# Six buffers for the split weights, and splits three quanta ahead of TensorE

## The reference

```python
xn = rmsnorm(x, norm_mix_pre)
p = (xn @ w_in).astype(f32)
p_rwkv, p_qkv, p_z, p_beta, p_alpha, p_gate_a, p_gate_b = _split(p, IN_SPLITS)
...
y = rwkv7_recurrence(rh, rwkv_heads(decay), kh, vh, -kk, kk * ah)
...
o = gated_delta_rule_chunked(q, k, gdn_heads(v), g, beta)
...
mixed = jax.nn.sigmoid(p_gate_a) * y_a + jax.nn.sigmoid(p_gate_b) * y_b
x = x + rmsnorm(mixed.astype(x.dtype) @ w_out, norm_mix_post)
xn = rmsnorm(x, norm_ffn_pre)
hidden = jax.nn.silu(xn @ ffn_w_gate) * (xn @ ffn_w_up)
return x + rmsnorm(hidden @ ffn_w_down, norm_ffn_post)
```

## Time and profile before

| what | us |
|---|---|
| median of 3 runs | 2353.65 |
| lowest and highest run | 2353.6 and 2360.31 |
| the profiled execution, its own time | 2358.39 |
| its span, first to last instruction | 2356.5 |
| PE busy | 2161.3 (92%) |
| DVE busy | 1414.1 (60%) |
| ACT busy | 1086.9 (46%) |

### The profile page before, as it was taken

One profiled execution on the slowest core, in us unless ns is written; L12 is line 12 of the kernel. 1 busy time (PEld: TensorE's weight loads), 2 busy tenths in 40 slices (PEclk: granted clock), 3 DMA queues, 4 the chain that ended last, 5 costly groups with the idle time before them and its releaser, 6 DMA issues. The chain is left out here.

```text
span 2356.5 us, 51465 instructions
## 1 busy us (share of the span) xinstructions
PE 2161.3 (92%) x19523; PEld 1862.1 (79%) x19523; DVE 1414.1 (60%) x2772; ACT 1086.9 (46%) x2019; POOL 158.2 (7%) x277
## 2 busy tenths in 40 slices
PE   5699999999999999999999966939999999999995
PEld 5698888888888888888888854838888888878884
DVE  3276687778677766867776754444554544444444
ACT  4354555545554545555454533344444444434443
POOL 2000110110011011101101110000000000000000
PEclk8699999999999999999999966969999999999998
DMA  4654545444444545444544304426655555545452
GB/s 114 155 143 116 138 111 132 123 125 125 115 116 123 129 113 139 113 113 123 130 114 113 87 5 185 154 90 197 195 182 192 181 192 182 174 165 191 178 184 101
DMA packets 388239, 327.32 MB, mean 139 GB/s; under 512 B 15360, under 2 KB 328160, under 8 KB 381408
## 3 DMA queue, kind: packets, MB, share of 16 engines
q1 hardware_dynamic: 376304, 319.16, 46.5%
q10 hardware_dynamic: 11760, 5.41, 0.9%
HBM read 322.44 MB, written 2.10 MB: 138 GB/s over the span
## 5 line engine op out<-in xcount | busy, mean ns | idle before, releaser
L1489 DVE TENSOR_TENSOR wlo<-wr,whi 128x1024 fp32r<-128x1024 f32 x296 | 362.4, 1225 | 436.0 <-ACT whi L1484 436.0
L232 PE MATMUL ps<-hi,xh 128*128 128x384 f32 (+1 forms) x1600 | 581.7, 364 | 42.8 <-DVE lo L218 24.4
L234 PE MATMUL ps<-hi,xl 128*128 128x384 f32 (+1 forms) x1600 | 548.9, 343 | 0.0
L233 PE MATMUL ps<-lo,xh 128*128 128x384 f32 (+1 forms) x1600 | 548.1, 343 | 0.0
L1484 ACT ACTIVATE whi<-wr 128x1024 fp32r<-128x1024 f32 x296 | 313.5, 1060 | 493.2 <-PE ps L1502 484.9
L218 DVE TENSOR_TENSOR lo<-raw,hi 128x768 fp32r<-128x768 f32 (+1 forms) x400 | 378.1, 964 | 147.6 <-ACT hi L213 144.0
L213 ACT ACTIVATE hi<-raw 128x768 fp32r<-128x768 f32 (+1 forms) x400 | 328.1, 834 | 245.8 <-PE ps L234 235.4
L232 PEld LDWEIGHTS ps<-hi,xh 128*128 128x128 f32 x1600 | 311.1, 194 | 76.4 <-issue 47.7
L1498 PE MATMUL ps<-whi,xh 128*128 128x512 f32 x832 | 328.1, 394 | 20.5 <-DVE wlo L1489 20.5
L1502 PE MATMUL ps<-whi,xl 128*128 128x512 f32 x832 | 326.9, 393 | 0.0
L1500 PE MATMUL ps<-wlo,xh 128*128 128x512 f32 x832 | 326.5, 392 | 0.0
(11 more groups left out here) (284 smaller groups left out, 2396.1 us busy)
## 6 DMA issues: line engine op xcount, KB each, us to landing
raw<-in_w_in SPq DMA_DIRECT2D x294, 512.0 KB, 5.5
wr<-in_ffn_w_gate SPq DMA_DIRECT2D x44, 1024.0 KB, 5.2
wr<-in_ffn_w_up SPq DMA_DIRECT2D x44, 1024.0 KB, 5.2
wr<-in_ffn_w_down SPq DMA_DIRECT2D x22, 2048.0 KB, 7.7
wr<-in_w_out SPq DMA_DIRECT2D x16, 1024.0 KB, 5.2
xt<-in_x SPq DMA_DIRECT2D x1, 2048.0 KB, 8.0
x<-in_x SPq DMA_DIRECT2D x1, 2048.0 KB, 15.8
out_x<-y SPq DMA_DIRECT2D x1, 2048.0 KB, 7.0
```

The lines of the kernel that those rows point to most:

```text
L232: nc.tensor.matmul(o, xh[:, kc, xs], hi[q % QBUF][:, k, 0:w], start=kc == 0, stop=False)
L233: nc.tensor.matmul(o, xh[:, kc, xs], lo[q % QBUF][:, k, 0:w], start=False, stop=False)
L234: last = nc.tensor.matmul(o, xl[:, kc, xs], hi[q % QBUF][:, k, 0:w], start=False, stop=kc == KC - 1)
L1489: nc.vector.tensor_tensor(wlo[s.par][:], src, whi[s.par][:].bitcast(F32), ALU.subtract).then_inc(s.lo, 1)
```

## The change

Two numbers are changed: `QBUF` from 4 to 6 and `LEAD` from 2 to 3. That gives two more tiles each of `hi` and `lo`, each of 2 x 384 float32 values in a partition. The function `held` is new: with six buffers the 16 quanta of the front stage are no multiple of the buffer count, so the quanta of the units are counted on from them.

```diff
-QBUF = 4
-LEAD = 2
+QBUF = 6
+LEAD = 3
...
+        def held(u, q):
+
+            return (q if u is None else QL + q) % QBUF
...
-            nc.scalar.activation(hi[q % QBUF][:, :, 0:w], raw_quantum(u, q, w), ACT.Copy).then_inc(hi_ready, 1)
+            nc.scalar.activation(hi[held(u, q)][:, :, 0:w], raw_quantum(u, q, w), ACT.Copy).then_inc(hi_ready, 1)
...
-            nc.vector.tensor_tensor(lo[q % QBUF][:, :, 0:w], raw_quantum(u, q, w),
-                                    hi[q % QBUF][:, :, 0:w].bitcast(F32), ALU.subtract).then_inc(lo_ready, 1)
+            nc.vector.tensor_tensor(lo[held(u, q)][:, :, 0:w], raw_quantum(u, q, w),
+                                    hi[held(u, q)][:, :, 0:w].bitcast(F32), ALU.subtract).then_inc(lo_ready, 1)
```

More of the change, by code:

```diff
@@ L231, in project @@
                     xs = slice(t * P, (t + 1) * P)
-                    nc.tensor.matmul(o, xh[:, kc, xs], hi[q % QBUF][:, k, 0:w], start=kc == 0, stop=False)
-                    nc.tensor.matmul(o, xh[:, kc, xs], lo[q % QBUF][:, k, 0:w], start=False, stop=False)
-                    last = nc.tensor.matmul(o, xl[:, kc, xs], hi[q % QBUF][:, k, 0:w],
+                    nc.tensor.matmul(o, xh[:, kc, xs], hi[held(u, q)][:, k, 0:w], start=kc == 0, stop=False)
+                    nc.tensor.matmul(o, xh[:, kc, xs], lo[held(u, q)][:, k, 0:w], start=False, stop=False)
+                    last = nc.tensor.matmul(o, xl[:, kc, xs], hi[held(u, q)][:, k, 0:w],
                                             start=False, stop=kc == KC - 1)
```

## The result

The changed kernel takes 2429.1 us (median of 4 runs, 2421.0 to 2430.4); the kernel before, run beside it, 2356.7 us. The ratio is 1.0305, with a 95% interval of 1.0282 to 1.0329. The prediction said 2354 us and no change. The profiled execution of the changed kernel took 2421.0 us, with a span of 2418.9.

What follows compares the result with a forecast made beforehand. The prediction took PE, busy 92% of the span, to bound the kernel, never waiting for a split in the loop. Every term was taken as 0, so the median stayed at 2353.65, say 2354 us; range 2349.2 to 2361.

Steps and rivals of the forecast that it cites:

- What bounds the kernel: Whole span: PE, busy 92%, waits for a `lo` only twice, 24.4 us, at the first quantum of a stage.
- Six buffers: Splits on ACT and DVE: waits on `quantum_done` are released earlier, no wait is added, PE gains nothing; worth 0.
- The copy out of PSUM: End of a pass: a split delays ACT's copy by at most 0.11 us; taken as 0, bound 1.5 us gained.
- the ends of the stage: Unit 0 makes one more split, the last unit one less; taken as 0, bound 0.96 us gained.
- Three ahead instead of two: Loop: more spare time between a `lo` and its use, loads start earlier but stay hidden; worth 0.
- With in-order queues that only release earlier, nothing behind a split can start later.: Queues of ACT, DVE and SP's loads: earlier releases delay nothing, so a loss is excluded.
- PE's waits in the loop: Units 1 to 14: `pu` 15.5 us, `yc` 6.5, top of loop 17.0; none is a split.
- The clock rival: Loop: half-clock stretches shift with PE's small steps; slower, 2371.9 us, chance 0.06, or faster, 2329.0 us, chance 0.04.
- What would show it: Profile after: PE's waits unchanged, ACT's split waits 177.5 to about 125 us, longer before `keep`, typical units 81.9 us.

Runs made afterwards that it cites:

- e1: Changed kernel with LEAD set back to 2, six buffers kept: 2350.0 us, ratio 0.9979.
- e3: Changed kernel with all six raw-weight loads of a unit released one quantum later, splits left alone: 2352.6 us, ratio 0.9994.
- e4: Changed kernel with only the second of a unit's six loads released one quantum later: 2350.5 us, ratio 0.9987.
- e5: Kernel before plus a spare 1.5 MB load per unit, one quantum before the second load, shortly before PE's jump: 2423.0 us, ratio 1.0302.
- e7: Changed kernel with two units in PE's loop body and 7 rounds instead of 14: 2389.2 us, ratio 1.0152.
- e12: Changed kernel with seven units in PE's loop body and 2 rounds, leaving one jump: 2345.4 us, ratio 0.9963.
- e6: Kernel before plus a spare 1.5 MB load per unit in the middle of PE's loop body: 2351.3 us, ratio 0.9995.
- e2: Kernel before with LEAD 3 and four buffers kept: 2523.4 us, ratio 1.0705.
- e9: Kernel before plus a spare 0.5 MB load per unit, before the second load, shortly before PE's jump: 2378.7 us, ratio 1.0107.
- e10: Kernel before with seven units in PE's loop body and 2 rounds, leaving one jump: 2342.9 us, ratio 0.9948.

## Why the prediction was wrong

The steps, as it put them:

- *What bounds the kernel.* Right. PE waits for a `lo` in the same two places, and for `pu` and `yc` as before.
- *Six buffers.* Right: no new wait of PE for a split or a copy came, and e1 shows the buffers free.
- *The copy out of PSUM, the ends of the stage.* 0 as taken; `pu` moved from 18.4 to 17.6 us.
- *Three ahead instead of two.* **This step failed.** It said: "the raw buffers are freed one quantum earlier too, so the loads start earlier", and that the loads are hidden before and after. It asked whether anyone waits for those loads, which nobody does (e3, e4), and not what else uses the DMA engines at the new time. The user was PE's instruction fetch. e4 and e5 show both directions: move this one load back and the loss goes, put another load at its place in the old kernel and the loss comes; e7 and e12 show that it takes PE's jump. What the step put at nothing came to 66.9 us in the loop: 38.5 us of standing still, and 28.4 us of clock.
- *"With in-order queues that only release earlier, nothing behind a split can start later."* No run speaks against it for the engines' own queues. But transfers share the DMA side, and in e5 and in the changed kernel an earlier load did delay another transfer, the fetch.
- *PE's waits in the loop.* The row for it was in the earlier trace rows: 17.0 us at the top of the loop, put down to "issue" or to `gb`. I listed it as not being a split and went on. A wait for issue on the engine that bounds the kernel had no cause in my account, so the claim that nothing could change it had no ground either.
- *The rivals.* The clock rival named the right sign and gave 2371.9 us at the worst. The clock did fall, from 0.98 to 0.95 over the loop, but not by the way it named, a shift in PE's small steps: 64.9 of the 71.7 us that were added at half clock amount to one new stretch at each jump. The kernel before and e1, e3, e4 and e6, whose jumps take 1.0 to 2.1 us, have none there; with 4.1 to 5.2 us every jump of the changed kernel has one. Right after a jump of the changed kernel the granted clock is half:

```profile
452.00:455.00 3.00, 2.96 (x16) 2.63 (x16) 0.85 (x2) 1.61 (x4) 0.00 (x0) 0.50 0.04 10
```

- *What would show it.* The fall of ACT's waits was forecast to 125 us and came to 87.5; the longer wait before `keep` was forecast and came (126.0). The counts that were to stay did stay. The sign that I named for a wrong forecast, units of another length, is what came: the units of the loop last 84 to 89 us, where 81.9 was typical.

What is still open: first, where the packet waits. In e2 1.5 MB were issued 3.8 us ahead, nearly as early as in the changed kernel, and the DMA engines were fuller, yet the packet came at -0.1 to +0.8 us and not at +1.3 to +2.5. So the bytes ahead alone don't set the delay, and no run tells the DMA engines from the memory behind them. Second, when a stretch at half clock comes: a jump longer by only 0.7 us brought them to six of e9's jumps and not to the others, and e10 has more of that time in the middle of units with no longer jump at all.

## What to carry to other kernels

When a change lets a transfer start earlier, look at what stands at its new time, not only at who waits for it. PE's loop has a moment at the jump in which PE needs the DMA engines itself; here a load that started with PE's last matmul was harmless, and the same load 4 us ahead cost 3%. The wait of the bounding engine that came back once per round and had no producer behind it was this jump. Seven units in PE's loop body brought 0.5% and all of them written out 0.7%, where two more buffers and one more quantum of lead brought nothing.

## What the runs showed of the hardware

- PE's first matmul behind a jump came 2.7 to 2.9 us after the start of the last 16 KB instruction packet, in 24 of 26 jumps, with the packet anywhere from 1.9 us before to 2.5 us after the start of the body's last matmul; 3.2 and 3.3 us in the other two. In the kernel before the packet starts 0.7 to 1.9 us before the body's last matmul, and from the start of that matmul to the next 1.6 us pass on average; with 1.5 MB issued 4.15 us ahead it is 4.6 us, with 0.5 MB issued 4.05 us ahead (e9) 2.4 us.
- Additional traffic of 1.5 MB per unit in the middle of the body was free (e6, 0.9995).
- The longer standstills cost PE more than their own time: 38.5 us came with 28.4 us of clock in the changed kernel, 9.3 us with some 19 us of clock in e9. A stretch at half clock stands at 0 of 13 jumps of 1.0 to 2.0 us (before), at 6 of 13 of 2.2 to 2.6 us (e9), and at 13 of 13 of 4.1 to 5.2 us (after).
